# Two units of the memory's keys moved out of the first mixer and split; high-part products ahead of the low ones

## What is computed

```python
h = rms_norm(x, norm_mix_pre); proj = h @ w_in              # q, k, v, u, 2 x 1024 gates
o_attn = stick_breaking_attention(q, k, v)                   # 8 heads
o_ssm = s5_branch(u, ...)                                    # complex linear recurrence, then a gated unit
merged = gate_attn * (o_attn @ w_branch_attn) + gate_ssm * (o_ssm @ w_branch_ssm)
x = x + rms_norm(merged @ w_out, norm_mix_post)
h = rms_norm(x, norm_xa_pre); mem_n = rms_norm(mem, norm_mem)
q, k, v = h @ xa_wq, mem_n @ xa_wk, mem_n @ xa_wv            # 4 heads over 256 memory rows
x = x + rms_norm(attention(q, k, v) @ xa_wo, norm_xa_post)
x = x + rms_norm(conv_ffn(rms_norm(x, norm_ffn_pre)), norm_ffn_post)
# second block
h = h + hybrid_mixer(rms_norm_2(h, norm1_g), ...)
h = h + hierarchical_moe(rms_norm_2(h, norm2_g), ...)        # 32 experts, top 2
return rms_norm_2(h, final_g)
```

## Time and profile before

| | |
|---|---|
| median of 3 runs | 1106.05 us |
| profiled execution | 1107.04 us, span 1105.3 us |
| TensorE matmul busy | 1077.1 us (97%) |
| VectorE busy | 616.9 us (56%) |
| ScalarE busy | 402.4 us (36%) |
| DMA, mean over the span | 274 GB/s |
| chain that ended last | TensorE 87%, DMA 6%, VectorE 4% |

### The profile page before, as it was taken

The page is one execution under the profiler, slowest core; times in us unless marked ns, Lnnn a source line. Parts: engine busy times, 40 slices in busy tenths (PEclk is TensorE's granted clock), DMA queues, the critical chain, the costliest instruction groups (busy, mean ns, idle before and its releaser), DMA issues.

```text
span 1105.3 us, 17603 instructions
## 1 busy us (share of the span) xinstructions
PE 1077.1 (97%) x7008; PEld 793.1 (72%) x7008; DVE 616.9 (56%) x1248; ACT 402.4 (36%) x650; POOL 6.0 (1%) x21
## 2 busy tenths in 40 slices
PE   8999999999999999999999999999999999999995
PEld 5988778998899999999799974444444444444442
DVE  4999997777568888788978651111111111112112
ACT  6512336466365555556685321111111111111112
POOL 2000000000000000000000000000000000000000
PEclk9999999999999999999999999999999999999999
DMA  8544323554245767675543699999999999999994
GB/s 301 172 162 143 105 86 115 172 172 134 76 153 185 239 227 253 229 261 173 190 153 123 248 406 408 421 420 421 420 421 420 421 420 420 420 421 420 421 419 178
DMA packets 56980, 302.63 MB, mean 274 GB/s; under 512 B 6592, under 2 KB 7744, under 8 KB 32320
## 3 DMA queue, kind: packets, MB, share of 16 engines
q1 hardware_dynamic: 53712, 287.60, 67.8%
q10 hardware_dynamic: 3184, 13.87, 3.5%
HBM read 300.39 MB, written 1.05 MB: 273 GB/s over the span
## 4 chain that ended last, share of the span: by engine, by line
PE 87%; DMA 6%; DVE 4%; ACT 1%; issue 1%; SPq 1%; DVEq 0%; ACTq 0%
PE psum L1937 86%; DMA arena<-in_experts 3%; DMA parts<-in_experts 3%; DMA ring<-in_stream 1%; DVE w_low L1113 1%; DVE arena L1113 1%; PE psum L2669 1%; ACT w_high L636 0%; DVE rt L1116 0%; DVE arena L1116 0%; DVE h L1116 0%; SPq L473 0%; PE psum L2675 0%; SPq L476 0%; DVE sq L1113 0%
## 5 line engine op out<-in xcount | busy, mean ns | idle before, releaser
L1937 PE MATMUL psum<-arena 128*64 128x512 f32 (+5 forms) x1488 | 265.4, 453 | 4.5 <-DVE scatter_turned L1109 1.1
L1937 PEld LDWEIGHTS psum<-arena 128*64 128x64 f32 (+2 forms) x1488 | 138.2, 160 | 132.5 <-issue 125.6
L1113 DVE TENSOR_TENSOR w_low<-ring,w_high 128x1024 fp32r<-128x1024 f32 x150 | 180.2, 1220 | 32.1 <-ACT w_high L636 31.6
L636 ACT CAST w_high<-ring 128x1024 fp32r<-128x1024 f32 x150 | 154.7, 1048 | 60.0 <-DMA ring<-in_stream 51.5
L1937 PE MATMUL psum<-h_high,w_high 128*128 128x256 f32 x528 | 150.4, 285 | 2.4 <-DVE w_low L1113 1.3
L1937 PE MATMUL psum<-h_low,w_high 128*128 128x256 f32 x528 | 148.3, 281 | 0.0
L1937 PE MATMUL psum<-h_high,w_low 128*128 128x256 f32 x528 | 148.3, 281 | 0.0
L1937 PE MATMUL psum<-y_high,w_high 128*128 128x256 f32 x480 | 135.0, 283 | 1.9 <-DVE w_low L1113 1.4
L1937 PE MATMUL psum<-y_high,w_low 128*128 128x256 f32 x480 | 133.9, 281 | 0.0
L1937 PE MATMUL psum<-y_low,w_high 128*128 128x256 f32 x480 | 131.4, 281 | 0.0
L1113 DVE TENSOR_TENSOR arena<-arena,psum 128x512 f32<-128x512 f32 (+1 forms) x31 | 19.4, 633 | 184.8 <-ACT arena L1051 184.0
(11 more groups left out here) (267 smaller groups left out, 1374.0 us busy)
## 6 DMA issues: line engine op xcount, KB each, us to landing
ring<-in_stream SPq DMA_DIRECT2D x180, 512.0 KB, 3.5
arena<-in_experts SPq DMA_DIRECT2D x90, 1024.0 KB, 26.2
parts<-in_experts SPq DMA_DIRECT2D x27, 1024.0 KB, 26.1
ring<-in_experts SPq DMA_DIRECT2D x27, 1024.0 KB, 26.4
spare<-in_experts SPq DMA_DIRECT2D x14, 1024.0 KB, 26.6
arena<-in_experts ACTq DMA_DIRECT2D x8, 1024.0 KB, 7.0
x<-in_experts SPq DMA_DIRECT2D x8, 1024.0 KB, 25.7
sq<-in_experts SPq DMA_DIRECT2D x7, 1024.0 KB, 26.4
```

Of the source, the lines that this page charges most:

```text
L636: act.copy(wh[:, high_slot(m)], ring[:, n_ % RING]).then_inc(hi_ready, 1)
L1113: return dve.tensor_tensor(o, a, b, op)
L1937: return pe.matmul(o, a, b, start=start, stop=stop, skip_group_check=True)
```

## The change

- The list of fillers has 22 units instead of 24: xk 6 and xk 7 leave it. Slots "table2" and (0, 1) hold two units instead of three, and all later fillers move up.
- xk 6 and xk 7 come behind xv 7 in the stream and are split. TensorE multiplies them with the memory's high and low parts (`yh`, `yl`) behind the values; ScalarE evicts them behind the values.
- Inside most units the matmuls with the weight's high part come first, behind a wait for the high part alone, and the matmuls with the low part follow, behind a wait of their own. Some units keep the joint wait: the first pair of "u" and of "out", four of "xo", the first five of the feed-forward stage, "v2", the last down unit and "out2".
- The expert slots on the high parts are listed in another order.

```diff
-LEFT = [("gate", i) for i in range(16)] + [("xk", i) for i in range(8)]
+LEFT = [("gate", i) for i in range(16)] + [("xk", i) for i in range(6)]
...
-UNITS += [("out", i) for i in range(8)] + [("xv", i) for i in range(4, 8)]
+UNITS += [("out", i) for i in range(8)] + [("xv", i) for i in range(4, 8)] + [("xk", i) for i in range(6, 8)]
...
-for slot, width in (("table", 1), ("table2", 3), ((0, 0), 2), ((0, 1), 3), ((0, 2), 2), ((1, 0), 1), ((1, 1), 2),
+for slot, width in (("table", 1), ("table2", 2), ((0, 0), 2), ((0, 1), 2), ((0, 2), 2), ((1, 0), 1), ((1, 1), 2),
                     ((1, 2), 1), ((2, 0), 1), ((2, 1), 2), ((2, 2), 1), ((3, 0), 1), ((3, 1), 2), ((3, 2), 1),
                     ("last", 1)):
...
-SPLITS = [key for key in UNITS if key[0] not in ("xk", "gate", "glu") and key not in UNITS[:4]]
+SPLITS = [key for key in UNITS if key[0] not in ("gate", "glu") and key not in UNITS[:4]
+          and (key[0] != "xk" or key[1] >= 6)]
...
-        held += [parts_double(2), ring_double(0), parts_double(4), ring_double(2), parts_double(0), ring_double(4)]
+        held += [parts_double(4), ring_double(0), parts_double(0), ring_double(2), parts_double(2), ring_double(4)]
...
-        fplan = [(("gate", i), "act") for i in range(8)] + [(("xk", i), "act") for i in range(4)]
+        fplan = [(("gate", i), "act") for i in range(8)] + [(("xk", i), "act") for i in range(3)]
...
-        pplan += [(("out", i), "act") for i in range(4)] + [(("xv", i), "act") for i in range(2, 4)]
+        pplan += [(("out", i), "act") for i in range(4)] + [(("xv", i), "act") for i in range(2, 4)] + [(("xk", 3), "act")]
...
             gained_inputs("xa_pre", hh, 0, 3)
             weights_high(UNIT_AT[("xq", 0)] + SPLIT_RING)
             evict_xv(1)
+            evict(("xk", 3), ("xk", 7), two(xkT, 3))
...
+            def high_part(key):
+
+                m = SPLIT_AT[key]
+                pe.wait_ge(hi_ready, m + 1)
+                return wh[:, high_slot(m)]
+
+            def low_part(key):
+
+                pe.wait_ge(lo_ready, SPLIT_AT[key] + 1)
+                return wl[:, UNIT_AT[key] % RING]
+
+            def rows_low(banks, key, src):
+
+                w_low = low_part(key)
+                for kk in range(2):
+                    k = 2 * (key[1] % 4) + kk
+                    for tt in range(TT):
+                        ins = mm(banks[tt][:], src[:, k, tt * P:tt * P + P], w_low[:, kk * 512:kk * 512 + 512], False,
+                                 k == KT - 1)
+                ins.then_inc(used, 1)
+
+            def rows_high(banks, key, src):
+
+                w_high = high_part(key)
+                for kk in range(2):
+                    k = 2 * (key[1] % 4) + kk
+                    for tt in range(TT):
+                        for part in src:
+                            mm(banks[tt][:], part[:, k, tt * P:tt * P + P], w_high[:, kk * 512:kk * 512 + 512],
+                               k == 0 and part is src[0], False)
...
             def split_tile_column(bank, key, i, c, src, ready, base):
-                w_high, w_low = split_unit((key, i if key in ("fg", "fv") else 2 * i + c))
+                name = key, i if key in ("fg", "fv") else 2 * i + c
+                o = bank[:, c * T:c * T + T]
+                w_high = high_part(name)
                 for k in range(KT):
                     if ready is not None and i == 0 and c == 0:
                         pe.wait_ge(ready, base + k + 1)
                     tile = slice(k * P, k * P + P)
-                    ins = mm_split(bank[:, c * T:c * T + T], (w_high[:, tile], w_low[:, tile]),
-                                   (src[0][:, k], src[1][:, k]), k == 0, k == KT - 1)
+                    mm(o, w_high[:, tile], src[0][:, k], k == 0, False)
+                    mm(o, w_high[:, tile], src[1][:, k], False, False)
+                w_low = low_part(name)
+                for k in range(KT):
+                    ins = mm(o, w_low[:, k * P:k * P + P], src[0][:, k], False, k == KT - 1)
                 ins.then_inc(used, 1)
...
             def split_rows(banks, key, src, first, end, ready=None, base=0):
                 for u in range(first, end):
+                    if ready is None:
+                        rows_high(banks, (key, u), src)
+                        rows_low(banks, (key, u), src[0])
+                        continue
                     w_high, w_low = split_unit((key, u))
...
                 for u in range(first, end):
-                    w_high, w_low = split_unit(("xv", 4 + u))
-                    for kk in range(2):
-                        k = 2 * u + kk
-                        for tt in range(TT):
-                            tile, columns = slice(tt * P, tt * P + P), slice(kk * 512, kk * 512 + 512)
-                            ins = mm_split(pb.bank(("xv", 2 + tt))[:], (yh[:, k, tile], yl[:, k, tile]),
-                                           (w_high[:, columns], w_low[:, columns]), k == 0, k == KT - 1)
-                    ins.then_inc(used, 1)
+                    banks = [pb.bank(("xv", 2 + tt)) for tt in range(TT)]
+                    rows_high(banks, ("xv", 4 + u), (yh, yl))
+                    rows_low(banks, ("xv", 4 + u), yh)
...
-            pe.wait_ge(*fb.read(("xk", 3)))
+            pe.wait_ge(*fb.read(("xk", 2)))
...
             def split_half_depth(bank, key, i, src):
-                w_high, w_low = split_unit((key, i))
+                w_high = high_part((key, i))
                 for c in range(2):
                     for k in range(4):
                         tile = slice((4 * c + k) * P, (4 * c + k + 1) * P)
-                        ins = mm_split(bank[:, c * T:c * T + T], (w_high[:, tile], w_low[:, tile]),
-                                       (src[0][:, k], src[1][:, k]), k == 0, k == 3)
+                        mm(bank[:, c * T:c * T + T], w_high[:, tile], src[0][:, k], c == 0 and k == 0, False)
+                        mm(bank[:, c * T:c * T + T], w_high[:, tile], src[1][:, k], False, False)
+                w_low = low_part((key, i))
+                for c in range(2):
+                    for k in range(4):
+                        tile = slice((4 * c + k) * P, (4 * c + k + 1) * P)
+                        ins = mm(bank[:, c * T:c * T + T], w_low[:, tile], src[0][:, k], False, k == 3)
                 ins.then_inc(used, 1)
...
             upper_values(0, 1)
             norm_spread(2)
             upper_values(1, 4)
+            pb.claim(pe, ("xk", 3))
+            split_cols_pair(pb.bank(("xk", 3)), "xk", 3, (yh, yl), None, 0)
...
             def down_unit(d):
+                b = d % 3
+                if d < FT - 1:
+                    w_high = high_part(("dn", d))
+                    pe.wait_ge(hid_ready, d + 1)
+                    for c in range(KT):
+                        o = pb.bank(("dn", c // 2))[:, (c % 2) * T:(c % 2) * T + T]
+                        mm(o, w_high[:, c * P:c * P + P], hh[:, b], d == 0 and c % 2 == 0, False)
+                        mm(o, w_high[:, c * P:c * P + P], hl[:, b], False, False)
+                    w_low = low_part(("dn", d))
+                    for c in range(KT):
+                        o = pb.bank(("dn", c // 2))[:, (c % 2) * T:(c % 2) * T + T]
+                        ins = mm(o, w_low[:, c * P:c * P + P], hh[:, b], False, False)
+                    ins.then_inc(used, 1)
+                    return
                 w_high, w_low = split_unit(("dn", d))
                 pe.wait_ge(hid_ready, d + 1)
-                b = d % 3
                 for c in range(KT):
                     tile = slice(c * P, c * P + P)
                     ins = mm_split(pb.bank(("dn", c // 2))[:, (c % 2) * T:(c % 2) * T + T],
                                    (w_high[:, tile], w_low[:, tile]), (hh[:, b], hl[:, b]),
-                                   d == 0 and c % 2 == 0, d == FT - 1)
-                    if d == FT - 1 and c % 2 and c < KT - 1:
+                                   False, True)
+                    if c % 2 and c < KT - 1:
                         ins.then_inc(dn_done, 1)
```

More of the change, by code:

```diff
@@ L2028, in split_rows @@
                     for kk in range(2):
                         k = 2 * u + kk
+                        pe.wait_ge(ready[0], base + k + 1)
                         for tt in range(TT):
                             tile, columns = slice(tt * P, tt * P + P), slice(kk * 512, kk * 512 + 512)
-                            ins = mm_split(banks[tt][:], (src[0][:, k, tile], src[1][:, k, tile]),
-                                           (w_high[:, columns], w_low[:, columns]), k == 0, k == KT - 1)
+                            mm(banks[tt][:], src[0][:, k, tile], w_high[:, columns], k == 0, False)
+                            mm(banks[tt][:], src[0][:, k, tile], w_low[:, columns], False, False)
@@ L2034, in split_rows @@
+                    for kk in range(2):
+                        k = 2 * u + kk
+                        pe.wait_ge(ready[1], base + k + 1)
```

(3 more changed lines are left out.)

11 lines of the change are left out of this document (removed).

## The result

| | before | changed |
|---|---|---|
| median | 1107.16 us, 6 runs (1105.7 to 1109.79) | 1112.91 us, 6 runs (1111.85 to 1116.44) |
| profiled execution | 1107.04 us, span 1105.3 | 1112.92 us, span 1111.1 |

The ratio is 1.0059, with a 95% interval of 1.0043 to 1.0074: the changed kernel is about 6.5 us slower by the ratio, 5.75 by these two medians. The forecast was 5.1 us, to 1111.2.

The account below looks back on a forecast made before the run. TensorE was taken to bound the dense half, with VectorE's recurrence just as full in the mixer, and DMA the experts. -1.65 + 5.70 + 1.95 - 0.52 - 0.35 = +5.1 us, to 1111.2; own range 1109.5 to 1113, overall 1107.5 to 1115.

Parts of the forecast that it names:

- Bound: Whole kernel: TensorE fills the dense half, DMA the experts; a microsecond won or lost before 650 us reaches the end whole.
- Part 1: Mixer: two filler units leave, but VectorE's recurrence holds the first outputs until 112.4 us, so only 1.65 us is gained.
- the two idles named: Mixer: VectorE's idles of 0.37 us and, at 135.22, 1.28 us, both expected to go.
- Part 2: Before the queries: the two units return as 48 split matmuls, +5.70 us, with nothing hiding them.
- Part 3: Ahead of the queries: ScalarE and VectorE stand until xq 1 lands; adding 5.4 us later, first scores +6.0 in all.
- the stall: At the queries: the late xq 1 load delays the queries' inputs, worth +1.95 us beyond the moved matmuls.
- Part 4: High products first: -0.52 us at xq 3, -0.35 at fg 3 and down unit 0, nothing at the start.
- The middle wait: Inside units, between high and low products: already met where the low part is ready, so it costs nothing.
- the fall in the mixer: Rival, chance 0.11: behind 112.4 us the clock halves over 3.7 us of work; +8.8 us, 1114.9.
- The rival without a stall: At the queries: the 5.70 us of new matmuls cover xq 1's late load; +3.2 us, 1109.2; chance 0.18.
- the one with a priced middle wait: In 126 units the wait between high and low products costs 0.07 us each; +8.8 us more, 1120; chance 0.08.
- the one in which the mixer follows TensorE: Mixer: all 7.1 us of removed filler come out instead of 1.65; -0.3 us, 1105.7; chance 0.05.

Follow-up runs that it names:

- the second profiles: The kernel before and the changed kernel each run again unaltered: 1106.29 us (ratio 0.9995) and 1113.43 us (ratio 1.0064).
- the doubling: Changed kernel with ScalarE's casts and VectorE's low parts ahead of the queries' inputs ending at xk 7, and the 48 last-keys matmuls issued twice: 1119.11 us, ratio 1.0104.
- the kernel with the later casts: Changed kernel with ScalarE's casts and VectorE's low parts ahead of the queries' inputs ending at xk 7 instead of xq 1: 1111.79 us, ratio 1.0041.
- the one with the high parts alone: Kernel before with the high products first and the two units still in the mixer: 1106.1 us, ratio 0.9993.
- the move without it: Changed kernel with the joint wait back in every unit, so only the two units are moved: 1114.58 us, ratio 1.0067.
- the last slots emptied: Changed kernel with query casts ending at xk 7 and the two fillers taken from slots (3, 2) and last instead: 1110.37 us, ratio 1.0031.

## Why the prediction was right, and where it was not

- *Bound.* The dense half's time reached the end: +5.97 at 520 us, +5.8 in the span. In the second profiles it is 525.73-520.82 = +4.91, and +4.7 in the span.
- *Part 1.* Outputs were forecast at 112.4; they started at 113.14, or 112.54 without the 0.60 of a later start, behind waits of 1.50 and 3.18 us (1.6 and 3.2 forecast). In the first profile the mixer gained 1.51 (1.65 forecast), by the two idles named. VectorE's 1.94 us ahead of the last outputs stayed 1.85.
- *Part 2.* 5.70 forecast, 5.73 measured by the doubling. "Nothing hides it" holds for the second set; the first also covers the waits that xq 0 has without it. From the landmark to the first scores, the kernel with the later casts takes 48.35 us and the one with the high parts alone 260.59-216.72 = 43.87: 4.5 more.
- *Part 3.* Adding forecast at 251.95, measured 252.86 (252.26 without the start); last low part of the inputs 260.95 against 261.85 (261.25). The first scores 266.05 against 266.89 (266.29). From the landmark behind the mixer to the first scores it is 266.89-215.78 = 51.11 us, 7.74 more than the 43.37 before, and parts 2 and 3 had 7.65. That path was read rightly. How it splits was not: without the stall 4.98 of the 7.74 are left (48.35), where the forecast had 5.70, and the stall is worth 2.6 us in the profile (about 2.0 by the ratios), where it had 1.95. The two misses cancel, since the stall's worth was what the path left over.
- *Part 4.* The wait at xq 3 went. The sum for the piece was 5.70+1.95-0.52 = 7.13; measured 7.11, and 112.86-105.88 = 6.98 in the second profile. But the -0.52 was put down to the products' order, and that isn't borne out: the order alone left the piece at 106.05 us, and the move without it had no wait at xq 3 either and took 112.92. At down unit 0 the wait changed its name as said: 353.99-328.77 = 25.22 against 25.52 before, -0.30 for -0.35. The middle wait was free: the kernel with the high parts alone, which has it in its units too, isn't slower than before.
- *The clock.* This is what the forecast got wrong. I gave the fall in the mixer 0.11 and a price of 3.7 us. It happened in six of seven profiles with these waits, and cost 1.61. The failing step was "idles such as the 1.41 us did not move it": one idle of 1.41 us behind long dense work said nothing of 1.50 and 3.18 us in a row. The sentence of the Trainium skill ("TensorE: Matmul & The Clock Gate", Part 1) that "activity releases the throttle" fits the runs better than my reading of the rows: where TensorE stayed busy from 104 to 112 us the clock never fell there. (In one of the seven it stayed up through the same waits.) The price was too high because the fall was shorter than I let it be: 3.7 us of matmuls at half the clock are 7.4 us, and in five of the six profiles with a fall it lasted 3.4. Where it lasted 6.8 us, it cost 3.0.

For a typical execution the sum is thus 5.1+1.6 = 6.7, against 6.5 and 7.1 by the two ratios. The forecast time was near because the path to the first scores was right to 0.1 us, and it was 1.7 us low: 1.1 by the base of three runs, the rest by the clock, as far as medians can tell. Some of the hit is luck: in six of the seven profiles the mixer's -1.65, a main term of the sum, was not there at all, and the measured 1112.91 lies just inside my own range, which ended at 1113. The rival without a stall, the one with a priced middle wait, and the one in which the mixer follows TensorE are each excluded by a run above.

## What to carry to other kernels

Taking work off an engine that only looks full opens waits, and the place that takes the work may have none: ask which engine ends the stage at the source, and what each instruction costs at the destination. A cast or preparation routine that works "up to unit n" must be looked at again whenever units are put in ahead of n; here that alone was 2.0 us by the ratios and 2.6 in the profile. When a wait is removed, name the next one on the same engine first, and see whether two short waits have become a long one.

## What the runs showed of the hardware

- The granted clock fell to 1.2 GHz behind one wait of 1.8 us in four of nine profiles of the same instructions, behind 1.5 (or 0.45) and 3.2 us in six of seven, behind 2.32 us in the one profile that had it, and behind the waits of 1.42, 1.16, 1.16 and 0.84 us in the one profile that had them. It stayed there for 3.4 us (in two falls for 6.8: with the keys twice, and behind those four waits), and cost the mixer about half of that: 1.61 and 3.0 us. One execution is no proof that a wait is harmless, or that it isn't.
- With the clock granted in full, the 1646 matmuls of the feed-forward stage took up to 3.6 us more or less, with the same waits among them: 195.7 and 197.5 us from spread to spread in two executions of the changed kernel, and 523.93-324.58 = 199.35 with the last slots emptied. What sets this is open.
